# The choice of experts for tile 3 in two halves, and the sample's attention one half block a step

## The reference

```python
q = (xb @ wq).reshape(n, 8, 2, 128)
sc = einsum("nhpc,hpkc->nhpk", q, subkeys)       # 8 heads, 2 lists of 128 scores each
s1, i1 = top_k(sc[:, :, 0], 16)
s2, i2 = top_k(sc[:, :, 1], 16)
cand = s1[..., :, None] + s2[..., None, :]       # 256 sums a head
cidx = i1[..., :, None] * 128 + i2[..., None, :]
top_s, pos = top_k(cand, 16)                     # 16 experts a head
eidx = take(cidx, pos)
g = softmax(top_s)
act = gelu(einsum("nhkd,nd->nhk", u[eidx], xb))
out = einsum("nhk,nhkd->nd", g * act, v[eidx])   # 128 experts for every row
```

## Time and profile before

| | |
|---|---|
| median of 3 runs | 2169.91 us (2168.32 to 2173.65) |
| the profiled execution | 2172.85 us, its span 2171.0 us |
| mean granted TensorE clock | 0.897 of full speed |
| busy: TensorE, VectorE, GpSimd, ScalarE | 1649.2, 1504.9, 750.6, 542.9 us |
| moved by DMA | 753.79 MB, mean 347 GB/s |
| gathers | 544, VectorE's dots 1.22 us each |

### The profile page before, as it was taken

The page is one execution under the profiler, slowest core; times in us unless marked ns, Lnnn a source line. Parts: engine busy times, 40 slices in busy tenths (PEclk is TensorE's granted clock), DMA queues, the critical chain, the costliest instruction groups (busy, mean ns, idle before and its releaser), DMA issues.

```text
span 2171.0 us, 22161 instructions
## 1 busy us (share of the span) xinstructions
PE 1649.2 (76%) x7163; PEld 1035.9 (48%) x7163; DVE 1504.9 (69%) x3350; ACT 542.9 (25%) x1451; POOL 750.6 (35%) x697
## 2 busy tenths in 40 slices
PE   7878889898878766988868667977886665666555
PEld 6777886375456522764466323535673222222211
DVE  1121207687877798458976898876789997888786
ACT  2233012111621222145601223733022210001011
POOL 0000000354333334334433334333254455554552
PEclk9988899999979987999989988987999888788878
DMA  7743564799999988999899988897999899999996
GB/s 229 264 140 97 202 229 162 291 421 396 423 369 421 421 347 344 370 387 347 331 417 421 419 300 362 333 410 298 420 379 421 330 413 410 422 421 421 422 403 275
DMA packets 129395, 753.79 MB, mean 347 GB/s; under 512 B 16992, under 2 KB 33296, under 8 KB 42880
## 3 DMA queue, kind: packets, MB, share of 16 engines
q0 software_dynamic: 78336, 570.46, 65.0%
q1 hardware_dynamic: 28432, 155.19, 19.1%
q10 hardware_dynamic: 22512, 26.73, 3.6%
HBM read 732.32 MB, written 19.48 MB: 346 GB/s over the span
## 4 chain that ended last, share of the span: by engine, by line
PE 38%; DMA 25%; DVE 25%; issue 6%; ACT 4%; POOL 1%; ACTq 0%; SPq 0%; DVEq 0%; POOLq 0%; PEldq 0%
DMA ring<-in_uv,stage 17%; PE pz L1249 8%; PE pz L1260 8%; DVE ring L1998 7%; PE acc L1598 7%; DVE vsum L2025 3%; DMA wbuf<-in_w_o 2%; DVE F L1875 2%; PE ps L1556 2%; PE ps L1501 2%; DMA wbuf<-in_w_q 2%; DMA wbuf<-in_w_pa 1%; DMA zt_joint<-F 1%; DVE F L1870 1%; PE ps L1521 1%
## 5 line engine op out<-in xcount | busy, mean ns | idle before, releaser
L804 POOL DMA_INDIRECT ring<-in_uv,stage x544 | 692.9, 1274 | 998.8 <-DVE vsum L2025 350.7
L1598 PE MATMUL acc<-ring,diag 128*128 128x512 f32 (+1 forms) x1112 | 623.0, 707 | 293.0 <-DVE diag L2009 202.9
L1998 DVE CUSTOM_DVE_ANT_0 ring<-ring,xb 128x1024 f32<-128x1024 f32 x544 | 649.3, 1221 | 95.0 <-DMA ring<-in_uv,stage 92.8
L1598 PEld LDWEIGHTS acc<-ring,diag 128*128 128x128 f32 (+1 forms) x1112 | 226.5, 217 | 651.8 <-DVE diag L2009 295.4
L2025 DVE SCALAR_TENSOR_TENSOR vsum<-ring,coefd,vsum 128x1024 f32<-128x1024 f32 x261 | 335.7, 1286 | 10.4 <-DVE coefd L2016 1.2
L1126 ACT ACTIVATE gel<-dots 128x1 f32<-128x1 f32 x544 | 102.0, 200 | 921.1 <-DVE dots L1998 907.0
L822 POOL COPY stage<-idx 128x4 int32<-128x4 int32 x136 | 54.9, 404 | 393.4 <-DVE gw L1944 392.6
L1249 PE MATMUL pz<-F,wbuf 128*128 128x128 f32 (+1 forms) x896 | 171.8, 351 | 9.8 <-PE pz L1249 4.8
L1249 PEld LDWEIGHTS pz<-F,wbuf 128*128 128x128 f32 x896 | 141.9, 200 | 40.0 <-issue 16.0
L2016 DVE TENSOR_SCALAR coefd<-gel,gw 128x1 f32<-128x1 f32 x266 | 55.8, 210 | 111.5 <-ACT gel L1126 111.2
L1260 PE MATMUL pz<-wbuf,F 128*128 128x256 f32 (+1 forms) x384 | 85.0, 381 | 1.9 <-PE pz L1260 1.9
(11 more groups left out here) (381 smaller groups left out, 1943.1 us busy)
## 6 DMA issues: line engine op xcount, KB each, us to landing
wbuf<-in_w_z SPq DMA_DIRECT2D x58, 1024.0 KB, 7.1
wbuf<-in_w_q SPq DMA_DIRECT2D x32, 1024.0 KB, 9.8
wbuf<-in_w_pa SPq DMA_DIRECT2D x16, 1024.0 KB, 10.0
wbuf<-in_w_o SPq DMA_DIRECT2D x16, 1024.0 KB, 10.3
ring<-in_uv,stage POOLq DMA_INDIRECT x544, 12.2
wbuf<-in_w_pb SPq DMA_DIRECT2D x16, 512.0 KB, 8.8
wbuf<-in_w_sk SPq DMA_DIRECT2D x4, 1024.0 KB, 11.0
zt_mid<-F ACTq DMA_DIRECT2D x18, 128.0 KB, 5.3
```

Of the source, the lines that this page charges most:

```text
L804: pool.indirect_dma_start(out=ring[:, slot, :], out_offset=None, in_=d["uv"], in_offset=bass.IndirectOffsetOnAxis(ap=stage[:, a, k:k + 1], ...
L1598: last = nc.tensor.matmul(acc[0:nq, c * 512:(c + 1) * 512], diag[:, parity, 0:nq], ring[:, slot, D + c * 512:D + (c + 1) * 512], start=Fal ...
L1998: nc.vector.tensor_tensor_reduce(out=u, in0=u, in1=xb[:, t % 2, :], scale=1.0, scalar=0.0, op0=ALU.mult, op1=ALU.add, accum_out=dots[:, sl ...
```

## The change

- Tile 3's choice is made for four heads at a time (JointTop, half 0 and 1). Half 0 takes the place of the whole choice beside tile 2's experts; its pieces weigh 1.0 in place of 1.5. Half 1 is a new kind of event, late_top, one piece every second pair of tile 3's experts, pairs 2 to 22.
- Tile 3's first 64 slots wait for half 0 (route_ready, t + 1), slot 64 of the tile for half 1 (t + 2); what came after counts one more.
- The sample's choice moves to every third pair, 26 to 56.
- The sample's attention turns and multiplies half block 2 in step 4 and half block 3 in step 5. Half block 3 uses the banks ps[0] and pz[0] in place of po, and its turn doesn't wait for the store before it. The stores of half blocks 2 and 3 come in steps 5 and 6.

```diff
     if i == JOINT or what == "sample":
-        return 1.5 if what == "front" and p >= TOP else 1.0
+        return 1.0
...
-        if 2 <= b < 2 + 4 * 11 and b % 4 == 2:
-            plan.append(("sample_top", TILES - 1, b // 4))
+        if 2 <= b < 2 + 2 * 11 and b % 2 == 0:
+            plan.append(("late_top", JOINT, b // 2 - 1))
+        if 26 <= b < 26 + 3 * 11 and b % 3 == 2:
+            plan.append(("sample_top", TILES - 1, (b - 26) // 3))
...
+class JointTop:
+    def __init__(self, M, half):
+        s0 = 2560 + 1024 * half
+        self.sc = M[:, s0:s0 + 1024].rearrange("p (k q) -> p k q", k=PC // 2)
+        self.onehot = M[:, s0:s0 + 1024].rearrange("p (s a) -> p s a", a=TOPK)
+        self.cand = M[:, 0:1024].rearrange("p (h a b) -> p h a b", h=HEADS // 2, a=TOPK)
...
+        def sample_tail(u):
+            return ps[0] if u == 3 else po
+
+        def sample_out(u):
+            return pz[0] if u == 3 else po
...
+                if b == SLOTS // BLOCK // 2 and h == 0 and t == JOINT:
+                    pool.wait_ge(route_ready, t + 2)
                 if b == 0 and h == 0:
-                    pool.wait_ge(route_ready, t + 1)
+                    pool.wait_ge(route_ready, t + 1 if t <= JOINT else t + 2)
...
-                for v in (u,) if u in (0, 1) else (2, 3) if u == 2 else ():
+                for v in (u,) if 0 <= u < 4 else ():
...
+            def late_top(t, i):
+                if i == 10:
+                    act.wait_ge(g_shift, t + 2)
+                    nc.scalar.activation(top_j[1].cand[:, :, 1, :], top_j[1].cand[:, :, 0, :], ACT.Exp).then_inc(g_exp, 1)
...
                     if u:
                         pe.wait_ge(turn_stored, 16 * t + u)
-                        pe.wait_ge(o_stored, 16 * t + u)
+                        if u < 3:
+                            pe.wait_ge(o_stored, 16 * t + u)
...
-                elif p == 4:
-                    for u in (2, 3):
-                        turn(u)
-                        pv(u)
+                elif p in (4, 5):
+                    turn(p - 2)
+                    pv(p - 2)
...
-                if u == 2:
-                    for w in (2, 3):
-                        dve.wait_ge(pv_done, 16 * t + w + 1)
+                if u in (3, 4):
+                    w = u - 1
+                    part = slice(DVB * (w - 2), DVB * (w - 1))
+                    dve.wait_ge(pv_done, 16 * t + w + 1)
...
-                a, heads = (fa(t), HEADS) if t <= JOINT else (top_s, HEADS // 4)
+                a, heads = (fa(t), HEADS) if t < JOINT else (top_j[half], HEADS // 2) if t == JOINT else (top_s, HEADS // 4)
...
+                elif what == "late_top":
+                    top(t, p, 1)
```

More of the change, by code:

```diff
@@ L423, in __init__ @@
         self.sc = M[:, 2560:4608].rearrange("p (k q) -> p k q", k=PC)
[L424 to L433, removed]
+class JointTop:
[4 more added lines that the diff above has]
+        self.cand = M[:, 0:1024].rearrange("p (h a b) -> p h a b", h=HEADS // 2, a=TOPK)
+        self.top1 = M[:, 2048:2176].rearrange("p (k s) -> p k s", k=PC // 2)
+        self.ix1 = M[:, 2176:2304].bitcast(U32).rearrange("p (k s) -> p k s", k=PC // 2)
+        self.ixf = M[:, 2304:2432].rearrange("p (k s) -> p k s", k=PC // 2)
+        self.top2 = M[:, 2432:2496].rearrange("p (h s) -> p h s", h=HEADS // 2)
+        self.pos2 = M[:, 2496:2560].bitcast(U32)
+        self.pa_u = self.pb_u = M[:, 2176:2240].bitcast(U32)
+        self.pab = M[:, 2240:2304]
+        self.e12 = M[:, 2048:2176].rearrange("p (b s) -> p b s", b=2)
 class SampleTop:
@@ L536, in build @@
         top_s = SampleTop(F, qT[:, D:D + 4 * P])
+        top_j = [JointTop(F, half) for half in range(2)]
         def fa(t):
@@ L1160, in _ @@
             load_x(1, 0)
-            act_stages = {"toeplitz": toeplitz, "bias": load_bias, "lambdas": lambdas, "load_x": load_x, "norm_h": norm_h, "turn_h": turn_h, "project": project, "front": front, "keep_h": keep_h, "load_h": load_h}
+            act_stages = {"toeplitz": toeplitz, "bias": load_bias, "lambdas": lambdas, "load_x": load_x, "norm_h": norm_h, "turn_h": turn_h, "project": project, "front": front, "keep_h": keep_h, "load_h": load_h, "late_top": late_top}
             for what, t, p in PLAN:
@@ L1444, in pv @@
                                 cols, v_ = slice(0, DVB), vb[0:w, j, h * DVB:(h + 1) * DVB]
-                            last = nc.tensor.matmul(po[DEC * i:DEC * i + DEC, cols],
+                            last = nc.tensor.matmul(sample_out(u)[DEC * i:DEC * i + DEC, cols],
                                                     joint.aTS[0:w, P * j + DEC * i:P * j + DEC * i + DEC], v_,
@@ L1882, in strike8, with top @@
                 step(last)
-            def top(t, i):
+            def top(t, i, half=0):
                 par = t % 2
-                a, heads = (fa(t), HEADS) if t <= JOINT else (top_s, HEADS // 4)
+                a, heads = (fa(t), HEADS) if t < JOINT else (top_j[half], HEADS // 2) if t == JOINT else (top_s, HEADS // 4)
+                turn = t + half if t <= JOINT else t + 1
                 lists, slots = 2 * heads, heads * TOPK
@@ L1938, in top @@
                                                         a.e12[:, 1, :], ALU.mult, ALU.add))
-                    step(nc.vector.tensor_copy(idx[:, par, 0:slots], a.e12[:, 0, :]))
-                    dve.wait_ge(g_exp, t + 1)
+                    here = slice(half * slots, half * slots + slots)
+                    step(nc.vector.tensor_copy(idx[:, par, here], a.e12[:, 0, :]))
+                    dve.wait_ge(g_exp, turn + 1)
                     gexp = a.cand[:, :, 1, :]
@@ L1943, in top @@
                     step(nc.vector.reciprocal(sstat[:, 0:heads], sst[:, 0:heads]))
-                    nc.vector.tensor_tensor(gw[:, par, 0:slots].rearrange("p (h s) -> p h s", h=heads), gexp,
+                    nc.vector.tensor_tensor(gw[:, par, here].rearrange("p (h s) -> p h s", h=heads), gexp,
                                             sstat[:, 0:heads].rearrange("p (h o) -> p h o", o=1)
@@ L2045, in experts @@
             def experts(t, b, h):
+                if b == SLOTS // BLOCK // 2 and h == 0 and t == JOINT:
+                    dve.wait_ge(route_ready, t + 2)
                 if b == 0 and h == 0:
-                    dve.wait_ge(route_ready, t + 1)
+                    dve.wait_ge(route_ready, t + 1 if t <= JOINT else t + 2)
                     if t == TILES - 1:
```

13 lines of the change are left out of this document (7 added, 6 removed).

## The result

| | before | after |
|---|---|---|
| median | 2169.17 us | 2144.74 us |
| all runs | 2168.32 to 2173.65 | 2141.25 to 2147.16 |
| ratio | | 0.9884, 95% interval 0.9863 to 0.9906 |
| profiled execution, span | 2171.0 us | 2145.3 us |

The change makes the kernel 1.16% faster, 24.4 us by the medians. The forecast was 14 us less, 2156; the measured median lies 2.3 us under the range. (The median of before has one run more in it here than in the table ahead of the prediction.)

The account below looks back on a forecast made before the run. Bytes set the pace, except where something keeps gathers from being issued. Choice -11, sample -7 and tile 3 +3.5 sum to -14.5 us, taking the median from 2169.91 to 2155.4, rounded to 2156; range 2147 to 2172.

Parts of the forecast that it names:

- The choice stretch: End of tile 3's choice beside tile 2's experts: 11 of 12 us lost DMA time won back, bounds 7 and 12.
- The half's price: VectorE's choice for four heads: 28.3 us, two halves 56.6 us, 3.7 more than one whole.
- The exponential's load: ScalarE, late half: two more table loads, measured 1.28 us each with no drain; by the skill page about 1.4 us more.
- The sample: Sample's attention, half blocks 2 and 3 in separate steps: 7 us of stall gone, bounds 0 and 12.
- no gap of 10 us between gathers there: Sign of a right forecast, in the sample's attention: GpSimd's gap of 10 us between gathers disappears.
- Tile 3: Second half beside tile 3's experts, slots 388 to 431: costs 3.5 us, bounds 0 and 9.
- Counted at nothing: Tile 2: eight slots moved to other stages, and VectorE's 8.6 us of added rows and diagonals, priced at no time.
- keeps its pace of one step for two slots: Tile 3's attention, 1340 to 1400: reading of its 18.5 us of lost DMA time.
- the list of places: Lost DMA time, 1314 to 1750: 18.5 us at attention, 16.2 at the sample, 12.0 at the choice; projections said to lose nothing.
- the GpSimd rival: Gather issues beside VectorE's choice in tile 3: GpSimd held up, 18 us too much, 2170 in all; chance 0.04.
- The rival "Larger": Choice and sample give all, 12 us each, and tile 3 hides its part: -24 us, 2146; chance 0.10.
- tile 3 turns bound by VectorE: Tile 3's experts: late pieces can't use idle time, costing 24.4 us; +6.4 or more in all, 2177; chance 0.10.

Follow-up runs that it names:

- late_crowded: Changed kernel with the second half's pieces beside every pair from 2 to 12 instead of every second one to 22; 2153.96 us, ratio 0.9922 to before.
- late_twice: Changed kernel with the costly instructions of the second half's choice, in tile 3, done twice; 2164.50 us, ratio 0.9988 to before.
- after_again: The changed kernel run once more, unaltered; 2151.31 us, ratio 0.9897 to before.
- weight_alone: Kernel before with only the weight of tile 3's whole-choice pieces set to 1.0, giving the changed kernel's spread beside tile 2; 2171.43 us, ratio 1.0001.
- open_alone: Kernel before with only tile 3's attention begun one pair later; 2166.32 us, ratio 0.9983.
- sample_alone: Kernel before with only the new steps of the sample's attention; 2166.81 us, ratio 0.9986.
- respread: Changed kernel with weights beside tile 2 of 1.15 for attention and the sample, 0.8 for the projections; 2148.09 us, ratio 0.9908 to before.

## Why the prediction was too careful

**The terms that were priced** came out together: half_wide is the change without the new spread of the pieces, and it gained 11.5 us by the medians and 17.2 - 5.4 = 11.8 us by its stages, 3 us less than the 14.5 of the sum.

**The choice stretch** (11 us, bounds 7 and 12): right. The lost time went from 12.4 to 1.5 us, at 413 GB/s.

**The half's price** (28.3 us, 56.6 for two): right to a tenth, 28.35 and 28.28.

**The exponential's load**: in after's trace of ScalarE the late one goes

```profile
1845.68 1.28 ACT L1144 ACT_TABLE_LOAD   x1
1846.98 0.26 ACT L1144 ACTIVATE F<-F 128x64 f32<-128x64 f32 x1
```

1.30 us from load to activation, and VectorE waited for it nowhere in tile 3. The drain that the Trainium skill adds to a load ("ScalarE: Activation LUTs", "What ACT_TABLE_LOAD costs") shows in no row here either.

**The sample** (7 us, bounds 0 and 12): right in kind, somewhat large: 5.1 us of lost DMA time, 2.5 us of tile 2 alone and 3 to 7 within after. The stage got one pair more by the plan (slots 294 to 311 in place of 292 to 307), so 2 slots and 5 us of bytes, not the 3 slots and 7.5 us of the prediction, and its sign "no gap of 10 us between gathers there" did not come: the 11.30 us above. 11.4 us of DMA time are still lost there.

**Tile 3** (3.5 us, bounds 0 and 9): right, 4.4 us, 3.0 against no late pieces at all. VectorE needed 6.4 us more up to slot 432 (the lower end of the 6.5 to 9.4), and was idle 7.3 us up to there in place of 20.3. late_crowded agrees with the cover of some 4 us that was read from the ring, and late_twice shows that after 28.3 us of work it is used up.

**What failed** is the term "Counted at nothing" for the eight slots that leave the choice, and with it the reading that tile 3's attention "keeps its pace of one step for two slots", so that its loss stays. The pace does stay, but the start doesn't. The 18.5 us at 1340 to 1400 were read as one kind of loss. In the first ten microseconds of that window, at a DMA share of 0.37, 7 us were lost for another reason: attention's first piece beside pair 2, right behind the finish, with TensorE's add held behind both and no gather for 16 us. By the plan's own arithmetic, which the prediction had, attention begins a pair later after the change. That is worth 7.2 us of lost time at the place. The projections' 5.5 us (at 1570 to 1600) were not on the list of places either; 4.8 of them went. Attention's extra pair took 2.6 back. So the term at nothing was worth 7.2 + 4.8 - 2.6 = 9.4 us. With it the account closes: the traces gained 22.2 us from slot 256 on (25.7 less the 3.5 before it; after_again's trace gives 20.4), 7.7 more than the 14.5 of the sum; the 9.4 less 1.9 for the sample and 0.9 for tile 3, plus 0.8 in tile 4, are 7.4. Shown are the sum of this term, by half_wide, which keeps the old spread and is 11 to 14 us slower than after by the ratios, and the wait at the opening, by 16 traces. How much each place is worth in the whole kernel is less sure: undoing the opening alone could not be told from after by the runs.

Smaller slips, which changed nothing: 2155.4 was rounded to 2156; and by the plan two pairs went to attention and the sample and two to the projections, not three and one. The equal medians of gather issues, 957 and 960 ns, by which the GpSimd rival was judged, are a weak sign: beside the choice (slots 344 to 375) other traces have medians up to 1359 ns, and the means in before are 1.25 us there and 1.15 us in slots 436 to 511.

**The rival "Larger"** (2146) came near the number for another reason. Both places giving all, 12 + 12 us, is not what happened, so that it lies 1 us from the measured median is luck. It gave VectorE's count as support, -23.4 us, but that count fails elsewhere: for half_wide it makes 24.6 + 7.4 = 32 us and tile 2 gained 17.2; for weight_alone it makes a loss of 8.6 and tile 2 gained 2.7. Lost DMA time per stage fits half_wide, reckoned afterwards: 12.4 of the choice and 5 of the sample are 17.4. The rivals by which tile 3 turns bound by VectorE, or GpSimd is held up, are out at 28.3 us of work.

Left open: why the projections lose 5 us and more in before, open_alone, sample_alone, half_wide and respread and next to nothing with after's spread, though the wait of 11.3 us stands in both; and what brings the granted clock, and with it 3 us, in attention up or down between executions of one plan.

## What to carry to other kernels

Where bytes set the pace, list the time that DMA loses stage by stage, over all stages, and price a change by which of those losses it can fill; taking work off an engine was worth no more here than the loss at that place (24.6 us of work, 12.4 won alone). When a plan spreads pieces by weight, recompute it for every stage before counting the rest at nothing: a piece moved by one pair at the opening took 5 to 10 us off that place, and thinning out the choice paid only together with halving it. Deferred work cost little here while VectorE stayed within what the gathers in flight cover (3.0 us of tile 3 for 28.3 us of work), and most of its length past that (17.5 for 19.9 more).

## What the runs showed of the hardware

The same code up to slot 256 took between 1303.9 and 1317.7 us in the 16 profiled executions, while with after's plan tile 2's 410 us repeated within about 4 us over six executions, and tile 3's 330 us lay between 329.1 and 331.6 over the eight whose code beside tile 3 is after's. Between 1330 and 1340 of before the granted TensorE clock was 0.50, behind a stretch in which TensorE had waited 8.26 us, and the same four matmuls took 2.08 us there and 1.13 us at full clock. Differences of about 5 us are better read from stage lengths in traces than from medians of whole runs, where the runs of one kernel spread over 5 to 18 us.
